# Log-decay sums of the decode rows: one row per batch and head, and one 256-column selector matmul per unit

## The reference, cut to what matters

```python
f_all = jnp.cumsum(jnp.concatenate([cache_fox_logf, logf], axis=1), axis=1)      # (8, 128+16, 8)
s = jnp.einsum('bqhd,bkhd->bhqk', q, k) * (D_F ** -0.5)
s = s + (f_all of the query  -  f_all of the key)                                 # per batch and head
s = jnp.where(qpos >= kpos, s, -inf);  p = softmax(s)
```

## Time and profile before

| | |
|---|---|
| median of 3 runs | 668.46 us (667.66 to 669.78) |
| span of the profiled execution | 665.6 us |
| PE busy | 634.8 us (95% of the span) |
| DVE, ACT, POOL busy | 348.1, 255.9, 124.5 us |
| DMA, mean over the span | 265 GB/s; 419 to 422 in most of the last stage's slices |
| `decay_sums` on PE | starts at 172.57 us |
| first and last decode unit | at 229.0 and 290.0 us |

### The profile page before, as it was taken

The page is one execution under the profiler, slowest core; times in us unless marked ns, Lnnn a source line. Parts: engine busy times, 40 slices in busy tenths (PEclk is TensorE's granted clock), DMA queues, the critical chain, the costliest instruction groups (busy, mean ns, idle before and its releaser), DMA issues.

```text
span 665.6 us, 9450 instructions
## 1 busy us (share of the span) xinstructions
PE 634.8 (95%) x3529; PEld 421.5 (63%) x3529; DVE 348.1 (52%) x737; ACT 255.9 (38%) x483; POOL 124.5 (19%) x138
## 2 busy tenths in 40 slices
PE   5999999998999999999999999999999999999985
PEld 4887888877888776778677878744434434443321
DVE  4649347994357565654356754656333433433212
ACT  5673343326334455565944324422211321212100
POOL 0018526663000310010000100022201401212111
PEclk9999999999999999999999999999999999999999
DMA  8975442363122833204967379999999999999991
GB/s 311 416 261 192 156 127 95 126 225 137 51 96 96 292 128 127 97 32 130 344 219 287 120 276 423 407 362 379 422 421 421 419 422 418 421 421 419 421 420 74
DMA packets 34721, 176.66 MB, mean 265 GB/s; under 512 B 4289, under 2 KB 4433, under 8 KB 21489
## 3 DMA queue, kind: packets, MB, share of 16 engines
q1 hardware_dynamic: 31696, 164.86, 63.6%
q0 software_dynamic: 2976, 11.16, 4.8%
HBM read 167.47 MB, written 9.06 MB: 265 GB/s over the span
## 4 chain that ended last, share of the span: by engine, by line
PE 70%; issue 9%; DMA 8%; ACT 4%; SPq 4%; DVE 4%; POOL 0%; POOLq 0%; ACTq 0%; DVEq 0%
PE banks L1620 13%; PE banks L1622 13%; PE banks L1621 13%; PE banks L1986 11%; DMA piece<-in_wexp 8%; PE banks L2009 5%; SPq L813 4%; PE banks L1972 2%; ACT z L1074 1%; PE banks L1827 1%; ACT w_hi L953 1%; PE banks L1906 1%; PE banks L1792 1%; PE banks L1799 1%; PE banks L1844 1%
## 5 line engine op out<-in xcount | busy, mean ns | idle before, releaser
L1188 DVE TENSOR_TENSOR w_lo<-raw,w_hi 128x1024 fp32r<-128x1024 f32 (+1 forms) x81 | 128.4, 1597 | 73.7 <-ACT w_hi L953 73.5
L1620 PE MATMUL banks<-w_hi,hT_hi 128*128 128x512 f32 x312 | 124.6, 399 | 2.4 <-ACT z L980 1.8
L1622 PE MATMUL banks<-w_hi,hT_lo 128*128 128x512 f32 x312 | 121.8, 390 | 0.0
L1621 PE MATMUL banks<-w_lo,hT_hi 128*128 128x512 f32 x312 | 121.6, 390 | 0.0
L1986 PE MATMUL banks<-piece,xs 128*64 128x512 f32 x512 | 116.3, 593 | 3.6 <-DMA piece<-in_wexp 3.1
L953 ACT ACTIVATE w_hi<-raw 128x1024 fp32r<-128x1024 f32 x79 | 83.5, 1057 | 90.7 <-PE banks L1622 86.6
L1986 PEld LDWEIGHTS banks<-piece,xs 128*64 128x64 f32 x512 | 37.1, 137 | 78.8 <-issue 70.8
L1620 PEld LDWEIGHTS banks<-w_hi,hT_hi 128*128 128x128 f32 x312 | 58.6, 188 | 15.7 <-issue 2.9
L1622 PEld LDWEIGHTS banks<-w_hi,hT_lo 128*128 128x128 f32 x312 | 58.6, 188 | 12.6
L1621 PEld LDWEIGHTS banks<-w_lo,hT_hi 128*128 128x128 f32 x312 | 58.7, 188 | 11.2
L2009 PE MATMUL banks<-piece,act_T 128*64 128x512 f32 x256 | 58.5, 598 | 1.3 <-DVE act_T L1417 0.3
(11 more groups left out here) (342 smaller groups left out, 952.9 us busy)
## 6 DMA issues: line engine op xcount, KB each, us to landing
piece<-in_wexp SPq DMA_DIRECT2D x96, 1024.0 KB, 20.0
raw<-in_wstream SPq DMA_DIRECT2D x79, 512.0 KB, 4.2
foxc<-in_foxc POOLq DMA_DIRECT2D x8, 512.0 KB, 5.9
memv<-in_memc SPq DMA_DIRECT2D x8, 512.0 KB, 4.8
memk<-in_memc SPq DMA_DIRECT2D x8, 512.0 KB, 4.9
xT<-in_xT SPq DMA_DIRECT2D x1, 1536.0 KB, 11.3
xtok<-in_xtok SPq DMA_DIRECT2D x1, 1536.0 KB, 8.0
x<-in_xtok SPq DMA_DIRECT2D x1, 1536.0 KB, 7.6
```

The costliest lines, as they stand in the source:

```text
L1188: dve.tensor_tensor(w_lo[:, i % PART_SLOTS, cols], raw[:, i % RAW_SLOTS, cols], w_hi[:, i % PART_SLOTS, cols].bitcast(F32), ALU.subtract). ...
L1620: mm(out, xh, wh, start=start, stop=False, skip_group_check=True)
L1621: mm(out, xh, wl, start=False, stop=False, skip_group_check=True)
L1622: return mm(out, xl, wh, start=False, stop=stop, skip_group_check=True)
```

## The change

The decode sums no longer stand on 8 partitions with one block of columns per batch, but with one row per batch and head: 64 rows, held twice (rows 0 to 63 the rounded values, rows 64 to 127 the remainders). `logc`, the cached log decays, is loaded twice side by side (128 columns), so that one matmul with `upper` gives all running sums of the caches, one with `ones` the whole sums, and one, with the new log decays repeated 16 times in `pick8`, adds the new ones. DVE keeps of the latter each row's own batch (constant `ownbatch`, which also negates). `nf_d` holds 128 columns for the cached keys and 128 for the new ones. A decode unit picks its eight rows with one matmul of 256 columns, whose stationary `rowsel[:, a, :]` is 128x128; POOL expands that table once, from 64 to 1024 columns, in `ret_state`. `ffw` shares its space with `logc`, for which SP waits. The space that the narrower `nf` leaves is not used.

```diff
-for _name, _n in (("ident", P), ("upper", P), ("ones", P), ("batchwin", 240), ("maskwin", 240), ("upper_in_batch", P),
+for _name, _n in (("ident", P), ("upper", P), ("ones", P), ("ownbatch", P), ("maskwin", 240), ("upper_in_batch", P),
...
-                  ("inbatch", NB), ("headsel", P), ("onehead", HF), ("pick", NI), ("rev4", T * 4), ("rev8", T * 8)):
+                  ("inbatch", NB), ("headsum", P), ("onehead", HF), ("rowsel", NB * HF), ("pick", NI), ("rev4", T * 4), ("rev8", T * 8)):
...
-        ffw = sm(64)
+        logc = sm(2 * NB * HF)
+        ffw = logc[:, 0:8 * KT]
...
-        nf = at("nf", [P, 256 + P + NB * P], o_sums, F32R)
-        nf_p, nf_n = nf[0:NF_ROWS, 0:256], nf[0:NF_ROWS, 256:384]
-        nf_c = nf[0:NF_ROWS, 384:].rearrange("p (b j) -> p b j", b=NB)
-        nf_hi, nf_lo = nf[0:8, :], nf[32:40, :]
+        nf_p = at("nf_p", [P, 256], o_sums, F32R)
+        nf_hi, nf_lo = nf_p[0:8, :], nf_p[32:40, :]
+        nf_d = at("nf_d", [P, 256], o_sums + KB, F32R)
...
+        rowsel = at("rowsel", [P, NB, P], o_work + 23 * KB, F32R)
...
                     elif i == 9:
                         load(const[:, :], io["const"], s_const_logc)
+                        sp.wait_ge(act_lo, 2 * KT + 1)
                         load(logc, io["logc"], s_const_logc)
...
                     act.wait_ge(sums_ready, 1)
-                    act.wait_ge(nf_zero, 1)
-                    act.activation(nf_hi[:, 0:384], ps[0:8, 3, 0:384], ACT.Copy, scale=-1.0)
-                    for q in range(2):
-                        ins = act.activation(nf_hi[:, 384 + 512 * q:896 + 512 * q], ps[0:8, 4 + q, :], ACT.Copy, scale=-1.0)
-                    ins.then_inc(sums_hi, 1)
+                    act.wait_ge(zeros_and_new, 2)
+                    act.activation(nf_hi, ps[0:8, 3, 0:256], ACT.Copy, scale=-1.0)
+                    act.activation(nf_d[:, 0:P], ps[:, 4, 0:P], ACT.Copy, scale=-1.0)
+                    act.activation(nf_d[:, P:256], pick8, ACT.Copy).then_inc(sums_hi, 1)
...
                     dve.scalar_tensor_tensor(logf, zf, 0.0, zl, ALU.min, ALU.subtract).then_inc(logf_ready, 1)
+                    dve.wait_ge(logf_ready, 1)
+                    dve.tensor_copy(pick8.rearrange("p (r h) -> p r h", h=HF), logf[:, 16:24].unsqueeze(1).to_broadcast([P, NI, HF])).then_inc(logf_ready, 1)
...
+                    dve.wait_ge(sums_ready, 1)
+                    dve.tensor_tensor(pick8, ps[:, 4, P:256], cst("ownbatch"), ALU.mult).then_inc(zeros_and_new, 1)
                     dve.wait_ge(sums_hi, 1)
-                    dve.scalar_tensor_tensor(nf_lo[:, 0:384], ps[0:8, 3, 0:384], -1.0, nf_hi[:, 0:384].bitcast(F32), ALU.mult, ALU.subtract)
-                    for q in range(2):
-                        cols = slice(384 + 512 * q, 896 + 512 * q)
-                        ins = dve.scalar_tensor_tensor(nf_lo[:, cols], ps[0:8, 4 + q, :], -1.0, nf_hi[:, cols].bitcast(F32), ALU.mult, ALU.subtract)
-                    ins.then_inc(sums_lo, 1)
+                    dve.scalar_tensor_tensor(nf_lo, ps[0:8, 3, 0:256], -1.0, nf_hi.bitcast(F32), ALU.mult, ALU.subtract)
+                    dve.scalar_tensor_tensor(nf_d[64:P, 0:P], ps[64:P, 4, 0:P], -1.0, nf_d[64:P, 0:P].bitcast(F32), ALU.mult, ALU.subtract)
+                    dve.tensor_tensor(nf_d[64:P, P:256], pick8[64:P, :], nf_d[64:P, P:256].bitcast(F32), ALU.subtract).then_inc(sums_lo, 1)
...
-            pool.memset(nf[:, :].bitcast(F32), 0.0).then_inc(nf_zero, 1)
+            pool.memset(nf_p[:, :].bitcast(F32), 0.0).then_inc(zeros_and_new, 1)
...
                     pool.wait_ge(s_state_out, 32)
+                    chain(pool.tensor_copy(rowsel[:, :, :].rearrange("p b (h i) -> p (b h) i", i=NI), cst("rowsel").unsqueeze(2).to_broadcast([P, NB * HF, NI])))
                     for b in range(2, 4):
                         store(foxc[fox_slot(b)][:, :], io["foxc"][b], foxc_in[fox_slot(b)])
...
-                    pe.wait_ge(logf_ready, 1)
+                    pe.wait_ge(logf_ready, 2)
...
-                    for b in range(NB):
-                        win = cst("batchwin")[:, (NB - 1 - b) * NI:(NB - 1 - b) * NI + P]
-                        mm(ps[0:8, 3, 256:384], logc[:, 8 * b:8 * b + 8], win, start=b == 0, stop=False, **kw)
-                    mm(ps[0:8, 3, 256:384], lf[2], cst("upper_in_batch"), start=False, stop=True, **kw)
-                    for b in range(NB):
-                        mm(ps[0:8, 4 + b // 4, (b % 4) * P:(b % 4) * P + P], logc[:, 8 * b:8 * b + 8], cst("upper"), start=True, stop=True, **kw)
+                    mm(ps[:, 4, 0:P], logc, cst("upper"), start=True, stop=True, **kw)
+                    mm(ps[:, 4, P:256], logc, cst("ones"), start=True, stop=False, **kw)
+                    mm(ps[:, 4, P:256], pick8, cst("upper_in_batch"), start=False, stop=True, **kw)
...
-                    mm(ps[:, 5, 0:P], headsel, nf_n, start=True, stop=True).then_inc(fqs_psum, 1)
+                    mm(ps[:, 5, 0:P], headsum, nf_d[:, P:256], start=True, stop=True).then_inc(fqs_psum, 1)
...
-                        mm(bank[:, 0:P], headsel, nf_c[:, a, :], start=True, stop=False, **kw)
-                        mm(bank[:, P:256], headsel, nf_n, start=False, stop=False, **kw)
+                        mm(bank[:, 0:256], rowsel[:, a, :], nf_d[:, :], start=True, stop=False, **kw)
```

More of the change, by code:

```diff
@@ L392, in program @@
         ss, rstd = sm(5), sm(5)
-        ffw = sm(64)
+        logc = sm(2 * NB * HF)
+        ffw = logc[:, 0:8 * KT]
         zf, zneg, ze, zl, logf = (sm(24) for _ in range(5))
-        logc = sm(64)
         fq_col = sm(16)
@@ L435, in program @@
         NF_ROWS = P
-        nf = at("nf", [P, 256 + P + NB * P], o_sums, F32R)
-        nf_p, nf_n = nf[0:NF_ROWS, 0:256], nf[0:NF_ROWS, 256:384]
-        nf_c = nf[0:NF_ROWS, 384:].rearrange("p (b j) -> p b j", b=NB)
-        nf_hi, nf_lo = nf[0:8, :], nf[32:40, :]
+        nf_p = at("nf_p", [P, 256], o_sums, F32R)
+        nf_hi, nf_lo = nf_p[0:8, :], nf_p[32:40, :]
+        nf_d = at("nf_d", [P, 256], o_sums + KB, F32R)
         sel = at("sel", [P, P + HF], o_sel, F32R)
-        headsel, onehead = sel[0:NF_ROWS, 0:P], sel[0:NF_ROWS, P:P + HF]
+        headsum, onehead = sel[0:NF_ROWS, 0:P], sel[0:NF_ROWS, P:P + HF]
         state = at("state", [P, 4, HR, P], o_work)
@@ L482, in program @@
         assert 12 * KB + 512 + 4 * NRT + 32 + 48 * T <= 18 * KB
-        const2 = at("const2", [P, N_CONST2], o_const + 4 * CONST["batchwin"][0])
-        assert CONST["batchwin"][0] + N_CONST2 <= CONST["decay_s"][0]
+        const2 = at("const2", [P, N_CONST2], o_const + 4 * CONST["ownbatch"][0])
+        assert CONST["ownbatch"][0] + N_CONST2 <= CONST["decay_s"][0]
         act_g = at("act_g", [P, 2, DE], o_ot)
@@ L541, in program @@
         tile_evac = [sem(f"tile_evac{t}") for t in range(2)]
-        nf_zero, sums_hi, sums_lo = sem("nf_zero"), sem("sums_hi"), sem("sums_lo")
+        zeros_and_new, sums_hi, sums_lo = sem("zeros_and_new"), sem("sums_hi"), sem("sums_lo")
         rank_tables = sem("rank_tables")
@@ L1001, in _ @@
                     act.wait_ge(sums_ready, 1)
-                    act.wait_ge(nf_zero, 1)
-                    act.activation(nf_hi[:, 0:384], ps[0:8, 3, 0:384], ACT.Copy, scale=-1.0)
-                    for q in range(2):
-                        ins = act.activation(nf_hi[:, 384 + 512 * q:896 + 512 * q], ps[0:8, 4 + q, :], ACT.Copy, scale=-1.0)
-                    ins.then_inc(sums_hi, 1)
-                    a = CONST["headsel"][0]
+                    act.wait_ge(zeros_and_new, 2)
+                    act.activation(nf_hi, ps[0:8, 3, 0:256], ACT.Copy, scale=-1.0)
+                    act.activation(nf_d[:, 0:P], ps[:, 4, 0:P], ACT.Copy, scale=-1.0)
+                    act.activation(nf_d[:, P:256], pick8, ACT.Copy).then_inc(sums_hi, 1)
+                    a = CONST["headsum"][0]
                     act.activation(sel[0:NF_ROWS, :], const[0:NF_ROWS, a:a + P + HF], ACT.Copy)
@@ L2066, in constants @@
     put("ones", np.ones((P, P)))
-    win = np.zeros((P, 240))
-    win[:, 112:128] = 1.0
-    put("batchwin", win)
+    put("ownbatch", -(((p % 64) // HF)[:, None] == b16[None, :]).astype(float))
     win = np.full((P, 240), -BIG)
@@ L2089, in constants @@
     put("inbatch", (b16[:, None] % 2 == np.arange(NB)[None, :]).astype(float))
-    put("headsel", ((b16[None, :] == p[:, None] % 32) & (p < 64)[:, None]).astype(float))
+    put("headsum", (b16[None, :] == p[:, None] % HF).astype(float))
+    put("rowsel", (np.arange(NB * HF)[None, :] == p[:, None] % 64).astype(float))
     put("onehead", ((np.arange(HF)[None, :] == p[:, None] % 32) & (p < 64)[:, None]).astype(float))
@@ L2157 @@
         "const": const, "const2": const2, "dtab": dtab, "qtab": qtab, "ffw": c(wff.reshape(KT, P, 8).transpose(1, 0, 2).reshape(P, 64)),
-        "logc": c(g["cache_fox_logf"][0].transpose(1, 0, 2).reshape(P, 64)), "wstream": c(np.concatenate(stream)),
```

(1 more changed line is left out.)

## The result

The changed kernel takes 663.35 us in the median (661.96 to 665.02, 4 runs), against 668.06 of the kernel before in the same comparison: a ratio of 0.9925, interval 0.9906 to 0.9945.

The account below looks back on a forecast made before the run. TensorE was taken to bound the kernel, with 70% of the chain at full clock. Decay sums 3.03 plus decode scores 0.5 made 3.5 us, giving a median of 665.0 us, range 663.5 to 666.8.

Parts of the forecast that it names:

- Does the gain reach the end?: From PE's granules to the last stage: the expert weight stream starts earlier by what PE won, so all 3.5 us arrive.
- The loads: SP's new wait ahead of logc costs nothing; logc grows by 32 KB, the constants shrink by 48 columns.
- Decay sums on PE: In decay_sums, 17 matmuls go and three with a 128-wide stationary come: 3.03 us saved, bounds 2.55 and 3.25.
- The lower bound: In decay_sums: wide loads don't overlap, each pass costs 0.19 us, six take 1.14, so only 2.55 us are saved.
- rival C: In decay_sums: wide loads don't overlap, so the sum is 3.05 us and the time 665.4; chance 0.06.
- Decode scores: Eight decode units on PE: one 256-column selector matmul for two of 128 saves 0.05 to 0.08 us each, 0.5 taken.
- The reading of the sums: DVE and ACT after decay_sums: 2.6 us against 3.2, still hidden by the granule between, so worth nothing.
- pick8: Copy into it on DVE behind the log decays: 0.1 us wait and 0.3 copy fit into 0.83 us idle.
- The selector table: POOL's expansion from 64 to 1024 columns takes 1.1 to 5.1 us, 1.1 taken; loses 0, or 0.7 at the upper end.
- Rival B: POOL's selector expansion is slow: gain gone at 8.0 us, at 10.2 the result is 670.8, slower; chance 0.03.

Follow-up runs that it names:

- sbuf192: Changed kernel with 192 unused bytes behind the constants in SBUF, putting later tiles at their addresses of the kernel before: 664.83 us, ratio 0.9947.
- before_aligned: Kernel before, without the change, with tiles behind the small ones moved 64 bytes so the pieces start on a multiple of 256: 665.63 us, ratio 0.9953.
- sbuf64: Changed kernel with 64 unused bytes behind the constants in SBUF, one write more per 8 KB row being one expectation: 664.41 us, ratio 0.9948.
- filler128: Changed kernel with 14 unused matmuls added to decay_sums, each with a stationary of 128 columns: 665.95 us, ratio 0.9963.
- two128: Changed kernel with each decode unit's 256-column selector matmul split again into two of 128 columns: 663.18 us, ratio 0.9918.
- expand3: Changed kernel with POOL's expansion of the selector table made three times: 661.83 us, ratio 0.9904.
- filler8: Changed kernel with 14 unused matmuls added to decay_sums, each with a stationary of 8 columns: 666.29 us, ratio 0.9971.
- after: The changed kernel itself, as first measured against the kernel before: 663.35 us, ratio 0.9925.
- after_again: Changed kernel measured once more, with no edit, as the repetition: 662.55 us, ratio 0.991.
- sbuf256: Changed kernel with 256 unused bytes behind the constants in SBUF, the pieces again on a multiple of 256: 662.1 us, ratio 0.9904.
- hbm: Changed kernel with the HBM arrays as large as before (constants padded, logc 64 columns loaded twice), SBUF unaltered: 662.97 us, ratio 0.9915.
- before: The kernel before, without the change: 668.06 us in the comparison with the changed kernel.
- sbuf128: Changed kernel with 128 unused bytes behind the constants in SBUF: 664.84 us, ratio 0.9953.

## Why the prediction was wrong

**Where it failed.** The step is "Does the gain reach the end?", with "The loads" before it: they follow the change's work into the last stage and take that stage as moved, not altered. I noted that the constants shrink by 48 columns and counted it as bytes to load. It was an address for everything behind. The term left out is 2.3 to 2.4 us: `sbuf192` takes it away from the changed kernel, `before_aligned` gives it to the kernel before. The size fits the rates: the end of the last stage waits for the stream of 96 pieces, and 84 pieces of 1.05 MB take 209 us at 421 GB/s and 2.5 us less at 426.

The Trainium skill has a rule that I should have weighed: "DMA: Bandwidth & Descriptors", section "How a descriptor splits into AXI transactions", says that a transaction has to start on a 256-byte boundary, so that a descriptor which does not start on one begins with a transaction from the boundary below it. The page words this for reads; here it is the side written, in SBUF, that was shifted. The runs agree on the boundary: 128 bytes past it is as bad as 64 or 192. They don't agree on the price: by my estimate from the page's beats, a row of 8192 bytes would cost 0.8% at 64 bytes and 2.3% at 192, and measured is 1.2% in every case. The 33 writes for 32 of `sbuf64`'s expectation would be 3%. What the DMA engines do with such a row, that it costs 1.2%, stays open.

**Decay sums on PE**: right. 3.03 forecast, 3.05 in the loads. The lower bound (0.19 a pass) is refuted by `filler128`, rival C with it. The rule on LDWEIGHTS that the prediction cites shows in the length of a record (0.10 us with 8 columns, 0.19 with 128) and hardly in the pitch (0.105 to 0.109, and 0.111), with 128 moving columns.

**Decode scores**: the mechanism right, the worth too high. 0.06 a unit stands in the trace as forecast, but 0.2 to 0.3 us in all reach the first piece, not 0.5: from the first retention score it is 209.0 us before (391.00 - 181.98), 208.7 after, 208.9 in `two128`. At one unit PE's selector load waits for ACT in all three (at 248.88 in the changed kernel), and `two128` loses nothing up to there from the unit before; where the rest goes is not shown.

**The reading of the sums, `pick8`, the loads' waits**: right, all hidden. The copy into `pick8` took 0.23 us, and DVE's `w_lo` behind it still waited 0.57 for ACT, for 0.83 before. The sums took 2.1 us from ACT's or DVE's first operation, 2.6 forecast.

**The selector table**: 1.88 us for 1.1, and harmless as forecast. The row of the same operation was the right one: undisturbed the copy takes 1.04 (`expand3`). What the prediction left out is that DVE can hold POOL as POOL holds DVE; it reckoned with the second alone. That `w_lo` is the cause is read from four copies in two traces, two of them beside it and long, two not; no run takes `w_lo` away. Rival B lay far off.

**The numbers**: 3.12 us ahead of the first piece, for a sum of 3.5; with the 2.4 of the layout that makes the spans' 5.5. That the forecast missed its range by only 0.15 us owes something to luck: its decode term, too high by 0.2 to 0.3, made up for a part of what was missing. And 0.4 us of the distance is not the change's: the kernel before was itself measured at 668.06 where the forecast starts from 668.46. In the repetition the miss is 0.95 us.

## What to carry to other kernels

Before costing an edit, list what it moves in memory: a table a few columns shorter shifts every tile laid out behind it, and stages that no line of the diff touches. Where a stage is limited by a stream of loads, look at the start of its destination rows modulo 256 bytes; here 64 bytes of padding in the kernel before were worth 2.4 us, and the rewrite itself 3.1. And compare the traffic line of the page slice by slice before looking for a cause in the edited code.

## What the runs showed of the hardware

- Rows of 8 KB (a piece) land at 426 GB/s when they start on a multiple of 256 bytes in SBUF, and at 421 when they start 64, 128 or 192 bytes past one. The front part of the kernel, where PE hardly waits for a load, didn't notice: the first piece went out at 387.7 to 388.4 in all layouts of the changed kernel.
- A matmul pass of fp32 with 128 moving columns has a pitch of 0.105 (`filler8`) to 0.109 us with a stationary of 8 columns and 0.111 with 128 (`filler128`); a change from 8 to 128 columns shows as a step of 0.22 once, the change back as one of 0.20 (`filler8`).
- POOL copied 128x1024 elements into fp32r in 1.04 us, and in 1.88 to 1.89 where DVE's `w_lo` (128x1024, two inputs in SBUF) ran beside it for 1 us (`after`, `expand3`). With the 0.824 us of a plain copy of 768 columns the undisturbed ones give 0.86 ns a column and 0.16 us once, an estimate from these two sizes.
- In part of the executions TensorE's granted clock falls to the lower level (1.2 GHz) for up to 7 us around the routing. Windows of such an execution of `after_again`: stretch, its length, busy time of PE, PEld, DVE, ACT, POOL, granted clock, DMA share, GB/s:

```profile
418.00:420.00 2.00, 1.52 (x14) 1.17 (x12) 1.58 (x4) 1.83 (x6) 0.00 (x0) 1.00 0.91 268
420.00:422.00 2.00, 2.00 (x20) 2.00 (x20) 1.66 (x12) 2.00 (x5) 0.00 (x0) 1.00 1.04 401
422.00:424.00 2.00, 2.00 (x8) 1.46 (x7) 1.37 (x9) 0.11 (x1) 0.00 (x0) 0.50 1.05 406
...
428.00:430.00 2.00, 2.00 (x8) 1.14 (x7) 0.17 (x2) 0.96 (x2) 0.00 (x0) 0.79 1.02 429
```

  Ahead of the fall PE has 0.48 us of idle time in one stretch of 2 us, in the midst of small matmuls (20 in the next 2 us). The profiled execution of the changed kernel has the same idle time there (1.52 us busy from 418 to 420) and keeps its clock, so what decides is not shown. From the first piece to the end, layouts on a multiple of 256 took 271.8 to 272.2 us at full clock (`after`, `filler8`, `expand3`), 272.9 where the clock was low for about half as long (`sbuf256`: 0.64 and 0.50 from 422 to 426), and 274.1 to 274.7 with the whole fall (`after_again`, `hbm`, `two128`, `filler128`, `before_aligned`). The others took 274.5 to 274.8 at full clock (`before`, `sbuf64`, `sbuf128`) and 276.9 with the fall (`sbuf192`). So the fall costs 2.3 to 2.4 us, the start off a multiple of 256 bytes 2.5 to 2.6, and both together 4.9: they add.
